# Norms of keys and queries over pairs of tiles, with the products of the inverse norms on ScalarE

## The reference, cut to what matters

```python
def _rms_norm(x, g):
    xf = x.astype(jnp.float32)
    y = xf * lax.rsqrt(jnp.mean(xf * xf, axis=-1, keepdims=True) + EPS)
    return (y * g.astype(jnp.float32)).astype(x.dtype)
...
    q = _rms_norm(zq.reshape(B, T, N_HEADS, HEAD_DIM), q_g)
    k = _rms_norm(zk.reshape(B, T, N_KV_HEADS, HEAD_DIM), k_g)
```

## Time and profile before

| | us |
|---|---|
| median of 3 runs | 1040.39 |
| lowest and highest | 1034.81, 1040.89 |
| the profiled execution | 1040.58 |
| its span on the core | 1038.8 |
| TensorE busy | 930.8 (90%) |
| VectorE busy | 694.0 (67%) |
| ScalarE busy | 372.5 (36%) |
| GpSimd busy | 85.4 (8%) |

### The profile page before, as it was taken

How to read it: one execution, slowest core, us unless ns; L and a number is a source line. 1 busy time by engine, 2 the same in 40 slices (tenths; PEclk the granted TensorE clock), 3 DMA queues, 4 the chain that set the end, 5 groups by cost and what they waited for, 6 DMA issues and landing times.

```text
span 1038.8 us, 11317 instructions
## 1 busy us (share of the span) xinstructions
PE 930.8 (90%) x3900; PEld 514.4 (50%) x3900; DVE 694.0 (67%) x1598; ACT 372.5 (36%) x830; POOL 85.4 (8%) x90
## 2 busy tenths in 40 slices
PE   3999999936899999999998899697598789999998
PEld 2866666713243444666643334353366555445432
DVE  5309987999896765888878889966487565432111
ACT  6310101102666656889700000122765364221000
POOL 0211010000541000000000000001011101310000
PEclk9999999877999999999999899788699789999999
DMA  8363020200662302001030000005012102320211
GB/s 291 108 188 62 1 81 3 83 0 1 203 210 83 112 34 84 26 22 61 0 102 21 21 20 12 0 1 210 21 52 61 31 11 62 104 100 31 71 62 42
DMA packets 35314, 69.82 MB, mean 67 GB/s; under 512 B 9609, under 2 KB 11953, under 8 KB 35249
## 3 DMA queue, kind: packets, MB, share of 16 engines
q1 hardware_dynamic: 28089, 43.93, 13.0%
q0 software_dynamic: 7168, 25.17, 7.4%
HBM read 58.46 MB, written 11.11 MB: 67 GB/s over the span
## 4 chain that ended last, share of the span: by engine, by line
PE 72%; DVE 21%; ACT 3%; issue 3%; DMA 1%; SPq 1%; DVEq 0%; ACTq 0%
PE ps L491 67%; DVE ctmp L1267 8%; PE ps L494 4%; DVE ct L1241 1%; DMA xn<-in_x_prompt 1%; DVE pv L1469 1%; ACT PTs L942 1%; ACT uT L1120 1%; DVE LB L1470 1%; DVE mcum L1395 0%; DVE zN L1493 0%; ACT relu L1058 0%; DVE pv L1435 0%; DVE uT L1675 0%; ACT sqj L955 0%
## 5 line engine op out<-in xcount | busy, mean ns | idle before, releaser
L491 PE MATMUL ps<-xT,W 128*128 128x344 f32 x960 | 283.8, 458 | 0.0
L491 PEld LDWEIGHTS ps<-xT,W 128*128 128x128 f32 x960 | 184.0, 193 | 97.6 <-issue 5.6
L491 PE MATMUL ps<-W,xT 128*128 128x512 f32 (+3 forms) x576 | 214.7, 531 | 1.2 <-ACT relu L1058 1.2
L1267 DVE SCALAR_TENSOR_TENSOR ctmp<-uT,chw,ctmp 128x1024 f32<-128x1024 f32 x116 | 152.0, 1310 | 4.1
L491 PEld LDWEIGHTS ps<-W,xT 128*128 128x128 f32 (+1 forms) x576 | 94.9, 185 | 113.7 <-issue 113.3
L1088 ACT ACTIVATE sgj<-SC,candn 128x1024 bf16<-128x1024 f32 (+3 forms) x128 | 114.5, 897 | 8.8 <-DVE candn L1373 6.6
L942 ACT ACTIVATE PTs<-ps 128x512 f32<-128x512 f32 (+3 forms) x96 | 43.1, 484 | 125.7 <-PE ps L494 125.7
L1706 DVE TENSOR_TENSOR ps<-ps,TP 128x256 f32<-128x256 f32 (+1 forms) x64 | 26.4, 412 | 71.2 <-PE ps L491 70.8
L1133 ACT ACTIVATE nsq<-ps 128x512 f32<-128x512 f32 (+1 forms) x18 | 10.7, 596 | 164.5 <-DVE nss L1482 120.9
L491 PE MATMUL ps<-kiT,qz 128*128 128x512 f32 (+3 forms) x160 | 61.7, 530 | 7.6 <-ACT relu L1058 6.5
L494 PE MATMUL ps<-Cc,Pm 128*128 128x128 f32 x288 | 46.6, 303 | 17.7 <-ACT PTs L942 17.5
(11 more groups left out here) (308 smaller groups left out, 1046.4 us busy)
## 6 DMA issues: line engine op xcount, KB each, us to landing
W<-in_w_in SPq DMA_DIRECT2D x8, 2048.0 KB, 8.7
xn<-in_x_prompt SPq DMA_DIRECT2D x8, 512.0 KB, 8.2
W<-in_w_out SPq DMA_DIRECT2D x1, 4096.0 KB, 13.3
resid<-in_x_prompt SPq DMA_DIRECT2D x16, 256.0 KB
out<-resid SPq DMA_DIRECT2D x16, 256.0 KB
out<-V SPq DMA_DIRECT2D x8, 256.0 KB
out<-zN SPq DMA_DIRECT2D x8, 256.0 KB, 2.0
bias_rows<-tprow SPq DMA_DIRECT2D x1, 1536.0 KB
```

The source lines that it names most:

```text
L491: return nc.tensor.matmul(out, lhsT, rhs, start=start, stop=stop)
L1267: ins = vec.scalar_tensor_tensor(conv[:, c, :] if j == CW - 1 else acc_, src, chw[:, c, j:j + 1], acc_, ALU.mult, ALU.add)
```

## The change

- VectorE's reduction of a tile writes columns 0 to 7 or 8 to 15 of `nss`; the chain of 12 runs once behind the reduction of each odd tile, on 128x16, and a memset raises `norms_ready`.
- The product with the inverse norms is now on ScalarE: `scaled(n)` multiplies eight 128x64 pieces, each by one column of `nrs`, drains the bank with the last, waits for that, and raises `z_scaled` with a copy of one element. Both tiles of a pair are scaled in ScalarE's even turn n + 2 behind that turn's square, the last pair behind the loop. `norm_out` is one turn later (n - 4), `squares` in turns 12 and 14 for 10 and 13.
- The product with the weight stays on VectorE for the nine k tiles and the sample rows of q (`gained`, three tiles behind). For the eight q tiles it goes into the eviction: `qgc` holds the weight of q twice over 128 partitions, times -64^-0.5, and is the scale of `norm_out`. Two small DMAs load it, one VectorE instruction scales it ahead of the page table's.
- TensorE's transposes are one turn later (n - 4), and those of q wait for `z_scaled`. Its other work keeps its turns. On VectorE `positions`, `pages`, `addresses`, `key_bias` and `center` are two turns later; the masks keep theirs.

```diff
@@ -278,12 +278,13 @@
     gqB = sb("gqB", [P, 2, HD], F32)
+    qgc = sb("qgc", [P, 1], F32)
     ss = sb("ss", [P, 16], F32)
...
     rtm = sb("rtm", [P, 16], F32)
-    nss = sb("nss", [P, 8], F32)
-    nrs = sb("nrs", [P, 8], F32)
-    ntm = sb("ntm", [P, 8], F32)
+    nss = sb("nss", [P, 16], F32)
+    nrs = sb("nrs", [P, 16], F32)
+    ntm = sb("ntm", [P, 16], F32)
     wI = sb("wI", [P, NT, 8], F32)
@@ -358,6 +359,10 @@
     zn_ready = sem("zn_ready")
+    norms_ready = sem("norms_ready")
+    z_scaled = sem("z_scaled")
+    q_gain = sem("q_gain")
+    q_gain_in = sem("q_gain_in")
     zn_out = [sem(f"zn_out{i}") for i in range(2)]
@@ -695,7 +700,7 @@
                 return
-            wait(zn_ready, n + 1)
+            wait(zn_ready if g == "k" else z_scaled, n + 1)
             o = begin(("tr", g, t), f"b{4 + n % 2}")
@@ -733,8 +738,8 @@
                 equal_before()
-            if n >= 3:
-                norm_transpose(n - 3)
+            if n >= 4:
+                norm_transpose(n - 4)
             if n == 3:
@@ -752,7 +757,7 @@
                 spread_rows(1)
-        for n in range(len(NORMED) - 3, len(NORMED)):
+        for n in range(len(NORMED) - 4, len(NORMED)):
             norm_transpose(n)
@@ -829,7 +834,7 @@
                 b = r // 2
-                wait(zn_ready, len(NORMED))
+                wait(zn_ready, NT + 2)
                 o = begin(("qb", b), "b7")
@@ -1105,8 +1110,27 @@
                     act.wait_ge(*plan.full(("vc", 1)))
+                if g == "q":
+                    act.wait_ge(q_gain, 1)
                 copy(dst[:, :, t * P:(t + 1) * P], pt(("tr", g, t)).rearrange("p (c n) -> p c n", c=4), ("tr", g, t),
-                     scale=1.0 if g == "k" else -HD ** -0.5)
+                     scale=1.0 if g == "k" else qgc[:, 0:1])
+
+        def scaled(n):
+            g, t = NORMED[n]
+            r = P if t < NT else NB
+            act.wait_ge(norms_ready, n // 2 + 1)
+            if n >= 2:
+                g2, t2 = NORMED[n - 2]
+                if t2 < NT:
+                    act.wait_ge(*plan.full(("tr", g2, t2)))
+                if g2 == "k":
+                    act.wait_ge(zn_out[n % 2], zn_stored(n - 2))
+            for h in range(H):
+                hs = slice(h * HD, (h + 1) * HD)
+                last = nc.scalar.activation(zN[0:r, n % 2, hs], pt(("z", g, t))[0:r, hs], ACT.Copy, scale=nrs[0:r, n % 2 * 8 + h:n % 2 * 8 + h + 1])
+            last.then_inc(plan.drain_sem(("z", g, t)), 1)
+            act.wait_ge(*plan.drained(("z", g, t)))
+            nc.scalar.activation(ss[0:NB, 15:16], ss[0:NB, 14:15], ACT.Copy).then_inc(z_scaled, 1)
 
@@ -1131,14 +1155,19 @@
             nc.scalar.activation(nsq[0:r, :], pt(("z", g, t))[0:r, :], ACT.Square).then_inc(nsq_done, 1)
-            if n >= 3:
-                norm_out(n - 3)
-            if n == 10:
+            if n >= 2 and n % 2 == 0:
+                scaled(n - 2)
+                scaled(n - 1)
+            if n >= 4:
+                norm_out(n - 4)
+            if n == 12:
                 squares(0, half_of(0), lnsq)
-            if n == 13:
+            if n == 14:
                 act.wait_ge(*plan.full(("vc", 0)))
                 squares(1, half_of(1), lnsq)
-        for n in range(len(NORMED) - 3, len(NORMED)):
+        scaled(len(NORMED) - 2)
+        scaled(len(NORMED) - 1)
+        for n in range(len(NORMED) - 4, len(NORMED)):
             norm_out(n)
@@ -1219,6 +1248,8 @@
 
+        v.wait_ge(q_gain_in, 32)
+        vec.tensor_scalar(qgc[:], qgc[:], -HD ** -0.5, None, ALU.mult).then_inc(q_gain, 1)
         v.wait_ge(pt_in, 32)
@@ -1477,21 +1508,25 @@
             r = P if t < NT else NB
-            z = pt(("z", g, t))[0:r, :].rearrange("p (h d) -> p h d", h=H)
+            c = n % 2 * 8
             v.wait_ge(nsq_done, n + 1)
-            vec.reduce_sum(nss[0:r, :], nsq[0:r, :].rearrange("p (h d) -> p h d", h=H), AXX).then_inc(nsq_used, 1)
-            v.wait_ge(nsq_used, n + 1)
-            link(vec.tensor_scalar(nss[0:r, :], nss[0:r, :], 1.0 / HD, EPS, ALU.mult, ALU.add))
-            rsqrt(nrs[0:r, :], nss[0:r, :], ntm[0:r, :])
+            vec.reduce_sum(nss[0:r, c:c + 8], nsq[0:r, :].rearrange("p (h d) -> p h d", h=H), AXX).then_inc(nsq_used, 1)
+            if n % 2:
+                v.wait_ge(nsq_used, n + 1)
+                if n >= 3:
+                    v.wait_ge(z_scaled, n - 1)
+                link(vec.tensor_scalar(nss[:], nss[:], 1.0 / HD, EPS, ALU.mult, ALU.add))
+                rsqrt(nrs[:], nss[:], ntm[:])
+                vec.memset(dsc[:, 7:8], 0.0).then_inc(norms_ready, 1)
+
+        def gained(n):
+
+            g, t = NORMED[n]
+            if (g, t) != ("q", NT) and g == "q":
+                return
+            r = P if t < NT else NB
             o = zN[0:r, n % 2, :].rearrange("p (h d) -> p h d", h=H)
-            if n >= 2:
-                g2, t2 = NORMED[n - 2]
-                if t2 < NT:
-                    v.wait_ge(*plan.full(("tr", g2, t2)))
-                if g2 == "k":
-                    v.wait_ge(zn_out[n % 2], zn_stored(n - 2))
-            vec.tensor_tensor(o, z, nrs[0:r, :].unsqueeze(2).broadcast_to([r, H, HD]), ALU.mult).then_inc(plan.drain_sem(("z", g, t)), 1)
-            v.wait_ge(*plan.drained(("z", g, t)))
+            v.wait_ge(z_scaled, n + 1)
             gain = gqB[0:r, 0 if g == "k" else 1, :].unsqueeze(1).broadcast_to([r, H, HD])
@@ -1523,6 +1558,8 @@
         for n in range(len(NORMED)):
+            if n >= 3:
+                gained(n - 3)
             norm(n)
@@ -1530,18 +1567,18 @@
                 ranks()
-            if 2 <= n <= 5:
-                for s in range(4 * (n - 2), 4 * (n - 1)):
+            if 4 <= n <= 7:
+                for s in range(4 * (n - 4), 4 * (n - 3)):
                     positions(s)
-            if 6 <= n <= 7:
-                pages(2 * (n - 6))
-                pages(2 * (n - 6) + 1)
-            if n == 7:
+            if 8 <= n <= 9:
+                pages(2 * (n - 8))
+                pages(2 * (n - 8) + 1)
+            if n == 9:
                 addresses()
-            if n == 8:
+            if n == 10:
                 for h in range(H):
                     key_bias(h)
-            if n == 9:
+            if n == 11:
                 center(0, 0, half_of(conv, 0), 512)
@@ -1555,11 +1592,14 @@
 
+        for n in range(len(NORMED) - 3, len(NORMED)):
+            gained(n)
+
         def decode_piece(n):
...
                 v.wait_ge(zs_in, 16 * 2)
-                v.wait_ge(zn_ready, len(NORMED))
+                v.wait_ge(zn_ready, NT + 2)
                 link(vec.memset(s64[:], 0.0))
@@ -1790,7 +1830,7 @@
             g.wait_ge(*plan.full(("tr", "q", k)))
-        g.wait_ge(zn_ready, len(NORMED))
+        g.wait_ge(zn_ready, NT + 2)
         for s in range(16):
@@ -1845,6 +1885,8 @@
         load_w(1)
+        for half in range(2):
+            sp.dma_start(qgc[64 * half:64 * half + 64, :], qg[0:1, :].rearrange("a d -> d a"), allow_slow_non_contiguous=True).then_inc(q_gain_in, 16)
         sp.dma_start(rb0[:, :], rel_bias[0:1, :].broadcast_to([NB, H])).then_inc(own_bias_in, 16)
```

## The result

| | before | changed |
|---|---|---|
| median, us | 1039.84 (4 runs) | 1063.45 (4 runs) |
| lowest and highest | 1034.81, 1040.89 | 1061.01, 1069.12 |
| profiled execution, its span | 1040.58, 1038.8 | 1069.12, 1067.3 |

The ratio is 1.0244, with a 95% interval of 1.0209 to 1.028: slower, by about 23.6 us of median. I had forecast slower, but 12.5 us, with 1061 as the upper end: the direction and the four places were right, the size was not.

A forecast was written before the change was run, and what follows sets the result against it. TensorE was taken as the bound, VectorE's work counting only where TensorE waits (21.3 us). Places 1 and 2 cancel to +0.4; with +5.1 and +7.0 that is 12.5 us on 1040.6: 1053.1 us, range 1044 to 1061.

The forecast's parts named there:

- What bounds the kernel: Norms of k and q: TensorE holds 72% of the chain; removed VectorE work is worth at most TensorE's 21.3 us waits.
- Place 1: Tiles 4 to 6: first pair's norms behind chosen(), rank counts behind three masks, so TensorE starts late; +9.5 us.
- Place 2: Tiles 6 to 14: 10.2 us key-bias wait goes, 3 us caught up, 4.6 us wait for squares comes; -9.5 us.
- Place 3: Turn 15: the variances wait for squares(1), behind scaled(13) and norm_out(10) on ScalarE; +5.1 us.
- Place 4: Last projection's end to first scores: 12.8 us instead of 5.8, with scaled tiles in ScalarE's queue; +7.0 us.
- from the scores to the end 322.5 us as now: Sign of a right forecast: the stretch behind the first scores keeps its length, 1038.8 - 716.3.
- The scaled tile: ScalarE's eight 128x64 products per tile: 2.0 us, bounds 1.05 and 2.75, with the marker 0.2 us after.
- my own scale (six tiles in all): Tile price counts once each in the first three places, three times in the fourth; 1.05 us a tile gives +7.4 us.
- A: Rival: VectorE was the bound and its removed work decides; places 3 and 4 under 3 us together, 1033 us; chance 0.08.
- B: Rival: no change seen, scaled tile near 1.3 us or TensorE's clock gives something back; 1048 us; chance 0.23.
- C: Rival: ScalarE becomes the bound in q at 2.75 us a tile; 1057.6 us, or 1059.5; chance 0.14.
- At nothing: Items costed at zero, chiefly the two qgc loads on SP's queue, covered by VectorE's 17.1 us wait before wrep.

The follow-up runs named there:

- e6: Kernel before with only q's weight moved into the eviction of the transposed queries, its loads and scale included; median 1037.3 us, ratio 0.9977.
- e1: Changed kernel with squares(1) back in ScalarE's turn 13, ahead of the products of tiles 12 and 13; median 1057.5 us, ratio 1.0164.
- e5: Changed kernel with the products of tiles 16 and 17 made on VectorE behind the last chain, not on ScalarE; median 1058.6 us, ratio 1.0176.
- e4: Changed kernel with five extra 128x512 matmuls ahead of each TensorE wait for the squares, results overwritten; median 1056.7 us, ratio 1.0156.

## Why the prediction was wrong, step by step

**What bounds the kernel.** Right: a long list of work taken from VectorE was worth nothing as such. 34 us went, and the stage grew. The one part that only removes VectorE work (e6) gave 1.2 us at the waits, not the 5.5 us of work that it removes.

**Place 1, predicted +9.5, measured +10.8.** Tile 4's projection is 4.8 us late, to a tenth as worked out, behind a wait for ScalarE's `zN`; the third rank row waits 4.03 us. The row starts 43.75 us after the first square, where the forecast had 43.8 (579.1); the excess is behind it, where the four instructions take 2.95 us and I had allowed 1.5. They stand first behind a wait too.

**Place 2, predicted -9.5 (-9.1 by its end at +0.4), measured -6.0** (tile 14: +4.8 after +10.8). The key-bias wait went and a wait for the squares came, 4.21 us for 4.6 said. The failing step is "So TensorE stands 2.0 + 0.2 + 2.2 (squares, 663.69) + latency = 4.6 us at that point": it prices the wait, and takes the 32 one-column matmuls behind it for the 3.63 us of the earlier trace rows. They took 6.99. That is +3.4 us. By its own terms (3 + 10.2 - 4.6) this place also came to -8.6 and not to -9.5 or -9.1.

Two more misses cancel inside this place, which is luck. From tile 6 to tile 12 TensorE caught up 1.0 us and not 3: the waits for `pv` and the rank rows behind them fell by 3.2 us, but the projections took 1.5 us more (8.87, 8.83 and 8.66 are long ones, where before there are two), and one tile's transposes more stand there. From tile 12 to tile 14 some 2 us fell away that I had not counted: with no 10.2 us wait ahead of it, tile 13's projection took 6.9 us for 8.2, and there are 0.8 us less of transposes.

**Place 3, predicted +5.1, measured +9.2.** The same omission: the wait is 4.77 us and the set again 6.99, +3.4; the projection between the places is 9.66 for 8.81, +0.85. e1 took the place away and gave back 10.0.

**Place 4, predicted +7.0, measured +6.8.** Right in size and cause; e5 showed 3.5 us of it to be ScalarE's two scaled tiles.

The excesses are 3.36 us for each set, 1.3 in place 1 and 0.85 for a projection, less a net 0.5 (the two waits are 0.4 and 0.3 us shorter than said and place 4 is 0.15, and 0.4 us is not accounted for): 8.3 us, the gap between 12.5 and 20.8. The mis-sized term is thus the price of a wait. I had used a long and a short projection for the state after a wait, from the earlier trace rows, but never asked it of the matmuls that stand first behind it; the clock of 0.80 in the earlier trace rows is a mean over 20 us of the kernel before, in which the set itself ran at 1.00, while in the changed kernel's sets it was 0.50 and 0.52. The 2 x 3.3 us are shown by e4, with the other engines' lists unchanged.

**Outside the stage.** With 20.8 for 12.5 us the sum would have been 1061.4; the median is 1063.45. The sign "from the scores to the end 322.5 us as now" failed too: it was 327.4, the same instructions at a granted clock of 0.59 for 0.71 in the first 40 us. I had put that at nothing, and its cause stays open.

**The scaled tile** was cheaper than the value taken: by the timeline 1.9 us with its marker for 2.2. By my own scale (six tiles in all) that should have brought some 1.8 us less; the waits of places 2 and 3 are 0.7 us shorter than said and place 4 is 0.15 under its forecast, and the rest I do not find. By the same six tiles the low end of the forecast, at 1.05 us a tile, is +6.8 and not +7.4.

**The rivals.** A fell: places 3 and 4 cost 16.0 us, where A needed under 3. B wanted a tile near 1.3 us, and it was 1.75 (1.9 with its marker); and the clock took rather than gave. C named a sum nearer the result (1057.6 to 1059.5) for a cause that is refuted: the tile was no dearer than 2.0 us but cheaper. **At nothing:** VectorE's first touch of `qgc` is at 30.45 us and waited for nothing.

Not tried: pairs of chains with the products kept on VectorE. Its product of the second tile of a pair would wait for transposes that stand behind rank rows, which wait for VectorE; that is argued, not shown.

## What to carry to other kernels

Work taken from an engine is worth what its waiters wait for, and here the order of three queues decided more than 34 us of work. Price a new wait of TensorE twice: its length, and the instructions that follow it at the lower clock (here +3.4 us on a set of 3.6, and 0.85 on the projection behind one of the two). When several products go to an idle engine, put what the critical engine waits for ahead of them; and mend neighbouring places together, since each alone only uncovers the other's wait.
